# Layer 0's memory projection in plain fp32 in a two-layer streaming encoder step, with its loads reordered

## The chip, the cores and the metric

The kernel runs on one core of a Trainium2 chip. The time is the device time of one execution in microseconds (us), with all inputs and outputs in HBM. Three executions of the kernel before took 2020.75, 2020.86 and 2020.9 us.

## What is computed

```python
for l in range(2):                                  # two layers
    z = x @ W_in[l]                                 # 512 prompt tokens + 32 sample tokens, width 2048
    mk, mv = split(mem @ W_mem_kv[l])               # 256 memory tokens, 4 key heads and 4 value heads of 128
    outs = fox(z), band(z), swa(z), cross(mq, mk, mv)   # four groups of four heads
    x = layer_norm(ALPHA * x + (concat(outs) * silu(gate)) @ W_out[l])
# x is layer-normed once before the first layer; mk and mv are outputs too
```

Everything is fp32 at the interface. The change touches `mem @ W_mem_kv[0]` and what runs beside it: the loads and the first layer norm of x.

## The kernel before, in words

All weights are stored as tiles of 128 output columns: `wt[n]` is 128 partitions x 16 contraction chunks x 128 columns, 1 MB, and goes into one of two slots of `WR`. A layer begins with eight such tiles for the memory (`MEM_TILES`), then come the heads' tiles.

A matrix product of fp32 precision is made of three products in fp32r, a reduced format that TensorE takes in one step. ScalarE casts a weight tile to its high part `WH` (`w_hi`, L730), VectorE subtracts it to get the low part `WL` (`w_lo`, L1046), and the memory is split in the same way into `MTH` (`mem_hi`, L859) and `MTL` (`mem_lo`, L1248). `mem_tile` (L672) then issues 48 matmuls of 128x128 weights against 256 columns: high x high, low x high, high x low, 16 chunks each, into one bank of `GB`. ScalarE copies the bank to `MT` (`mem_done`, L907) and issues the store of a key head. Value heads are transposed by `turn_mem` (L638).

Each engine runs an order written out by hand: `PE_PLAN`, `ACT_PLAN` and `DVE_PLAN`. Beside the eight memory tiles, layer 0 does the first layer norm with tokens as rows: five row blocks `XT` (the last, 32 rows, is `XTS`) are loaded (L374), summed (`first_sum`, L916 on ScalarE, L1311 on VectorE), squared (`first_square`, L923), turned to 1/deviation (`first_seed` L929/L931, `first_rstd` L1324 to L1328) and normalised (`first_norm`, L1333). Then TensorE transposes them chunk by chunk inside memory tiles 5, 6 and 7 (`turn_x`, L648 and L654, at the places that `TURNED` names), VectorE scales them (`first_affine`, L1351), and ScalarE casts them and stores them (`first_hi`, L942 and L944), two chunks for each `("x", g)` of the plan. After tile 7, `forget` (L619, L626) computes the forget gates from all 16 casted chunks; it waits for `xh` to count 16.

In `mem_done(0, j)` ScalarE waits for the end of tile j, casts the weights of tile j + 2 (which waits for their load), and only then copies tile j's bank:

```python
act.wait_ge(zd, n + 2)
if j < MEM_TILES - 1:
    w_hi(n + 2, s, l * (LT // 2) + j // 2 + 2)
...
act.copy(MT[:, s, :], GB[:, 2 * s, 0:NMEM]).then_inc(zf[s], 1)
```

All loads here are issued by SyncE, in order; a wait holds up everything behind it. A slot of `WR` may be loaded again when `w_lo` of the tile in it is done (`lo`). POOL issues the stores of the value heads. Tile n begins when its bank of two is free (`zf`), so ScalarE may be one tile behind. The order of loads is: tile 0's weights, the memory in quarters, row block 0, tile 1, row block 1, tile 2 (after tile 0 is split), row blocks 2, 3 and 4, the identity and norm vectors, tile 3, the other constants, and the later tiles in a loop.

Layer 1 does its memory tiles in the same way, beside another norm; the change leaves them alone but for their counts.

Of the kernel before, what the change touches and what calls it, by code (L numbers as in the profile page):

```python
# [14 lines left out]
KC = DM // P  # L15
# [4 lines left out]
NMEM = 256  # L20
# [20 lines left out]
WT = O0 + KC  # L41
# [9 lines left out]
class Group:  # L51
    def __init__(self, blocks, cached, own, place, sink=False):
# [23 lines left out]
    [("w1", 0), ("sum", 0), ("square", 0), ("mem", 0), ("square", 1), ("square", 2), ("mem", 1), ("square", 3),  # L76
     ("square", 4), ("seed", 0), ("mem", 2), ("mem", 3), ("mem", 4), ("sample", 0), ("x", 0), ("x", 1), ("x", 2),
     ("mem", 5), ("x", 3), ("x", 4), ("x", 5), ("mem", 6), ("x", 6), ("x", 7), ("mem", 7)],
# [3 lines left out]
    [("w1", 0), ("sum", 1), ("sum", 2), ("w", 0), ("sum", 3), ("sum", 4), ("w", 1), ("rstd", 0), ("norm", 0),  # L82
     ("w", 2), ("norm", 1), ("norm", 2), ("norm", 3), ("norm", 4), ("w", 3), ("sample", 0), ("x", 0), ("x", 1),
     ("w", 4), ("x", 2), ("mv", 4), ("x", 3), ("w", 5), ("x", 4), ("x", 5), ("mv", 5), ("x", 6), ("x", 7), ("w", 6),
     ("low", 0), ("low", 1), ("low", 2), ("low", 3), ("low", 4), ("mv", 6), ("low", 5), ("low", 6), ("low", 7),
     ("mv", 7)],
# [55 lines left out]
def encoder_step(nc, wt, wff, bff, x_t, mem_t, fox_k, fox_v, fox_logf, band_k, band_v, swa_k, swa_v, mem_k, mem_v,  # L142
                 rel_pad, sinks, ln_gt, ln_bt, ident_d, causal_d, swa_mask_d, cos_d, sin_d,
                 y_o, fk_o, fv_o, fl_o, bk_o, bv_o, sk_o, sv_o, mk_o, mv_o):
    with ExitStack() as ctx:
# [14 lines left out]
        def sem(name):  # L160
            return ctx.enter_context(nc.semaphore(name))
# [96 lines left out]

        hi = sem("hi")
# [93 lines left out]

        def pt_col(j):
            return PT[:, P * j:P * (j + 1)]
# [10 lines left out]
        def _(sp):  # L366

            sp.dma_start(WR[:, 0, :, :], wt[0]).then_inc(raw[0], 16)
            for p in range(NQ):
                cs = slice(p * KC // NQ, (p + 1) * KC // NQ)  # L370
                sp.dma_start(MTR[:, cs, :], mem_t[:, cs, :]).then_inc(ld_mem[p], 16)
# [31 lines left out]

            for l in range(DEPTH):
                load_weights(2 if l == 0 else 0, O0 // 2, l * LT, l * WT)
                for h in range(2):
                    load_weights(0, KC // 2, l * LT + O0 + h * KC, l * WT + O0)
# [8 lines left out]
        def _(pe):  # L416
# [240 lines left out]
            def mem_tile(l, j, turned, middle=None):  # L657
                s, n = j % 2, l * LT + j
                pe.wait_ge(hi, n + 1)
                pe.wait_ge(zf[s], l * (LT // 2) + j // 2 + 1)  # L660
                for i, (w, x) in enumerate(((WH, MTH), (WL, MTH), (WH, MTL))):
                    if i == 1:
                        pe.wait_ge(lo, n + 1)
                    for k in range(KC):
                        at = i * KC + k
                        if j == 0 and k % (KC // NQ) == 0 and i != 1:
                            pe.wait_ge(m_lo if i else m_hi, NQ * l + k // (KC // NQ) + 1)
                        if at % 3 == 0 and at // 3 in turned:
                            turn_x(turned[at // 3])
                        if at == 3 * KC // 2 and middle is not None:  # L670
                            middle()
                        mm = pe.matmul(GB[:, 2 * s, 0:NMEM], w[:, s, k, :], x[:, k, :],  # L672
                                       start=(at == 0), stop=(at == 3 * KC - 1))
                mm.then_inc(zd, 1)

            pe.wait_ge(s_one, 1)
            for l in range(DEPTH):
# [7 lines left out]
                for kind, i in PE_PLAN[l]:  # L685
                    if kind == "mem":
                        mem_tile(l, i, TURNED.get(i, {}) if l == 0 else {}, last_sums if l and i == 0 else None)
# [36 lines left out]
        def _(act):  # L724
# [221 lines left out]
            w_hi(0, 0, 1)  # L946
            mem_hi(0)
            act.wait_ge(s_one, 1)
            act.preload_act_table_set("natural_log_exp_and_others")
            for l in range(DEPTH):  # L950
                for kind, i in ACT_PLAN[l]:
                    if kind == "w1":
                        w_hi(1, 1, 1)
                    elif kind == "sum":
# [86 lines left out]
        def _(dve):  # L1041
# [202 lines left out]
            def mem_lo(r):  # L1244
                for p in range(NQ):
                    cs = slice(p * KC // NQ, (p + 1) * KC // NQ)
                    dve.wait_ge(m_hi, NQ * r + p + 1)
# [115 lines left out]
            for released, count in ((zd, 1), (zf[0], 1), (zf[1], 1), (tf, 1), (gd, 1), (oe, 2), (pv, 2), (sm1, 1),  # L1363
                                    (sm2, 2)):
                dve.sem_inc(released, count)
# [3 lines left out]
            w_lo(0, 0)  # L1369
            mem_lo(0)  # L1370
            chains = {"first": Chain(dve, c_dx), "ln": Chain(dve, c_dl), "ff": Chain(dve, c_df), "pair": Chain(dve, c_dc)}
            heads_chain = chain
            for l in range(DEPTH):
                chain = chains["ln" if l else "first"]
                for kind, i in DVE_PLAN[l]:
                    if kind == "w1":
                        w_lo(1, 1)
                        first_mean(0)
# [316 lines left out]
```

## Time and profile before

| | us |
|---|---|
| three executions, median | 2020.86 |
| the profiled execution | 2021.17 |
| its span in the profile | 2019.4 |
| TensorE busy (98% of the span) | 1981.5 |
| VectorE busy | 1049.7 |
| ScalarE busy | 705.0 |

The span is what the hardware profiler records of one execution; about 1.8 us of the time lies around it. Positions below are us from the start of the span. Of a matmul, the duration includes its way through the array, so consecutive ones overlap: the distance from one to the next is what a stream costs, and the chain of waits shows that. The granted clock is 1.00 where TensorE runs at 2.4 GHz and 0.50 where it runs at 1.2 GHz.

### The profile page before, as it was taken

Reading aid. Unit: us, or ns where it says so; the run is one execution under the profiler, and the core shown is the slowest. Engines: PE = TensorE matmul, PEld = TensorE weight load, DVE = VectorE, ACT = ScalarE, POOL = GpSimd, SP = SyncE. Lnnn points to the kernel's source line nnn. Section 1 sums busy time; section 2 is a strip of 40 time slices with the busy share of each in tenths; the row PEclk is TensorE's granted clock in tenths of the full one; section 3 lists DMA queues with packets and bytes.
Section 4 is the critical chain, followed back from the end, with each engine's and each line's share of the span. In section 5 each row is a group of like instructions: output and inputs, shape, how many; then the busy total and the mean of one; then the engine's idle time right before and its main releaser. Section 6 shows DMA issues by size and latency. Waiting matters only on the chain.

```text
span 2019.4 us, 38302 instructions
## 1 busy us (share of the span) xinstructions
PE 1981.5 (98%) x15868; PEld 1956.7 (97%) x15868; DVE 1049.7 (52%) x1649; ACT 705.0 (35%) x1053; POOL 133.4 (7%) x238
## 2 busy tenths in 40 slices
PE   7999999999999999999999999999999999999995
PEld 6999999999999999999999999999999999999995
DVE  6743333333465445677884333434335545557776
ACT  6423232222233233544573222222222322344444
POOL 0110000000000000000001101000000000000000
PEclk9999999999999999999999999999999999999998
DMA  8632232222222222555664323222222222225563
GB/s 305 241 131 93 98 107 85 99 99 90 94 71 99 69 90 82 201 201 194 220 216 142 107 88 107 84 100 86 91 105 90 79 72 87 100 72 211 182 225 133
DMA packets 55050, 254.75 MB, mean 126 GB/s; under 512 B 9468, under 2 KB 19324, under 8 KB 30864
## 3 DMA queue, kind: packets, MB, share of 16 engines
q1 hardware_dynamic: 31184, 202.68, 28.0%
q0 software_dynamic: 13344, 36.51, 5.3%
q10 hardware_dynamic: 10432, 14.29, 1.9%
q8 instruction: 65, 1.06, 0.2%
q14 instruction: 25, 0.20, 0.0%
HBM read 228.36 MB, written 27.70 MB: 127 GB/s over the span
## 4 chain that ended last, share of the span: by engine, by line
PE 96%; DVE 2%; DMA 1%; ACT 1%; issue 0%; SPq 0%; ACTq 0%; DVEq 0%
PE GB L426 62%; PE GB L450 19%; PE AB L479 3%; PE AB L522 3%; PE GB L672 3%; PE AB L490 2%; DMA WR<-in_wt 1%; PE AB L619 1%; DVE WL L1046 1%; PE AB L527 0%; PE AB L507 0%; PE AB L530 0%; PE AB L626 0%; PE AB L654 0%; PE AB L494 0%; DVE OY L1287 0%
## 5 line engine op out<-in xcount | busy, mean ns | idle before, releaser
L730 ACT CAST WH<-WR 128x2048 fp32r<-128x2048 f32 x184 | 351.2, 1908 | 725.7 <-PE GB L426 531.3
L1046 DVE TENSOR_TENSOR WL<-WR,WH 128x2048 fp32r<-128x2048 f32 x184 | 421.4, 2290 | 344.3 <-ACT WH L730 344.0
L426 PE MATMUL GB<-XH,WH 128*128 128x272 f32 x3328 | 458.1, 290 | 0.0
L426 PE MATMUL GB<-XL,WH 128*128 128x272 f32 x3328 | 451.3, 287 | 0.0
L426 PE MATMUL GB<-XH,WL 128*128 128x272 f32 x3328 | 451.2, 287 | 0.0
L426 PEld LDWEIGHTS GB<-XL,WH 128*128 128x128 f32 x3328 | 431.2, 189 | 0.0
L426 PEld LDWEIGHTS GB<-XH,WL 128*128 128x128 f32 x3328 | 431.2, 189 | 0.0
L426 PEld LDWEIGHTS GB<-XH,WH 128*128 128x128 f32 x3328 | 429.5, 188 | 1.5
L450 PE MATMUL GB<-XH,WL 128*128 128x272 f32 x1024 | 149.7, 288 | 3.3 <-DVE WL L1046 3.3
L450 PE MATMUL GB<-XL,WH 128*128 128x272 f32 x1024 | 151.3, 288 | 0.0
L450 PE MATMUL GB<-XH,WH 128*128 128x272 f32 x1024 | 149.2, 287 | 0.0
L743 ACT ACTIVATE S<-S,nmx 128x256 f32<-128x256 f32 (+8 forms) x160 | 83.8, 524 | 174.4 <-DVE nmx L1088 172.7
L450 PEld LDWEIGHTS GB<-XH,WL 128*128 128x128 f32 x1024 | 136.4, 188 | 4.2 <-DVE WL L1046 4.2
L450 PEld LDWEIGHTS GB<-XL,WH 128*128 128x128 f32 x1024 | 137.1, 188 | 0.5
L450 PEld LDWEIGHTS GB<-XH,WH 128*128 128x128 f32 x1024 | 136.3, 188 | 0.0
L1153 DVE SCALAR_TENSOR_TENSOR SPL<-GB,SPL 128x544 fp32r<-128x544 f32 x24 | 17.3, 720 | 141.6 <-ACT SPL L789 141.6
L1119 DVE SCALAR_TENSOR_TENSOR GA<-ES,GB 128x544 f32<-128x544 f32 x30 | 21.6, 719 | 119.6 <-ACT ES L758 119.6
L1105 DVE COPY PT<-AB 128x512 f32<-128x512 f32 x64 | 40.2, 670 | 68.8 <-PE AB L490 68.8
L1088 DVE TENSOR_REDUCE nmx<-S 128x1 f32<-128x256 f32 (+8 forms) x160 | 69.8, 436 | 5.5
L479 PE MATMUL AB<-SPL 128*128 128x256 f32 (+6 forms) x552 | 70.3, 279 | 0.0
L479 PEld LDWEIGHTS AB<-SPL 128*128 128x128 f32 (+1 forms) x552 | 64.7, 164 | 4.1
L522 PE MATMUL AB<-PT,V 128*128 128x128 f32 x560 | 67.6, 275 | 0.0
(178 smaller groups left out, 1496.3 us busy)
## 6 DMA issues: line engine op xcount, KB each, us to landing
WR<-in_wt SPq DMA_DIRECT2D x184, 1024.0 KB, 4.8
XR<-out POOLq DMA_DIRECT2D x64, 136.0 KB, 2.9
out<-OY ACTq DMA_DIRECT2D x24, 272.0 KB, 2.2
out<-OY ACTq DMA_DIRECT2D x8, 544.0 KB, 5.4
out<-KT POOLq DMA_DIRECT2D x16, 272.0 KB, 2.5
out<-VT POOLq DMA_DIRECT2D x16, 272.0 KB, 2.3
XT<-in_x_t SPq DMA_DIRECT2D x4, 1024.0 KB, 13.5
BI<-nc_rows POOLq DMA_DIRECT2D x8, 400.0 KB, 4.2
```

What stands on the lines that cost most here:

```text
L426: mm = pe.matmul(GB[:, 2 * s + hf, 0:HALF], w[:, s, k, :], x[:, k, hf * HALF:(hf + 1) * HALF], start=(k == 0 and i == 0), stop=(k == KC - ...
L450: mm = pe.matmul(GB[:, 2 * s + hf, 0:HALF], w[:, s, k, :], x[:, k, half(hf)], start=(at == 0), stop=(at == 3 * KC - 1))
L479: mm = pe.matmul(AB[0:r, b, at:at + w], q[:, t0:t0 + r], k, start=(p == 0), stop=(p == 2))
L490: mm = pe.transpose(AB[:, j // 4, P * (j % 4):P * (j % 4 + 1)], S[:, at:at + P], ident[:, :])
L522: mm = pe.matmul(AB[:, 3, P * i:P * (i + 1)], V[:, kb, :], pt_col(j), start=(b == 0), stop=(b == len(g.blocks[i]) - 1))
L672: mm = pe.matmul(GB[:, 2 * s, 0:NMEM], w[:, s, k, :], x[:, k, :], start=(at == 0), stop=(at == 3 * KC - 1))
L730: act.copy(WH[:, s, :, :], WR[:, s, :, :]).then_inc(hi, 1)
L743: act.activation(s, s, ACT.Exp, bias=nmx[0:r, i:i + 1], accum_out=esum[0:r, i:i + 1]).then_inc(ex, 1)
L1046: dve.tensor_tensor(WL[:, s, :, :], WR[:, s, :, :], WH[:, s, :, :].bitcast(F32), ALU.subtract).then_inc(lo, 1)
L1088: dve.tensor_reduce(nmx[0:r, i:i + 1], S[0:r, at:at + w + g.sink], AX_X, ALU.max, negate=True).then_inc(mk, 1)
L1105: dve.tensor_copy(PT[:, 512 * b:512 * b + w], AB[:, b, 0:w]).then_inc(pte, 1)
L1119: dve.scalar_tensor_tensor(split2(GA[:, :]), split2(ES[:, :]), 1.0, z2(s), ALU.add, ALU.mult) \
```

## The change

Layer 0's memory tiles are no longer split. A new `first_mem_tile` multiplies the loaded weights `WR` with the loaded memory `MTR`, 16 matmuls per tile, both operands plain fp32. ScalarE's `w_hi` and `mem_hi` and VectorE's `w_lo` and `mem_lo` of these tiles are gone; `hi` and `lo` are set to 8 at the start instead. The splits of tiles 8 and 9, the first of the heads, stay where they were (in `mem_done(0, 6)`, and in the first head).

A slot of `WR` is now free when its tile's matmuls are done: the loads of tiles 2 to 9 wait for `zd`. The first load becomes four quarters, each followed by a quarter of the memory; tile 1 goes ahead of row block 0; tile 3 goes ahead of the identity and norm vectors. `turn_x` keeps its positions in `TURNED`, which now count the 16 matmuls of a tile (before: every third of 48).

```diff
@@ ACT_PLAN and DVE_PLAN, layer 0
-    [("w1", 0), ("sum", 0), ("square", 0), ("mem", 0), ("square", 1), ("square", 2), ("mem", 1), ("square", 3),
...
+    [("sum", 0), ("square", 0), ("mem", 0), ("square", 1), ("square", 2), ("mem", 1), ("square", 3), ("square", 4),
...
-    [("w1", 0), ("sum", 1), ("sum", 2), ("w", 0), ("sum", 3), ("sum", 4), ("w", 1), ("rstd", 0), ("norm", 0),
-     ("w", 2), ("norm", 1), ("norm", 2), ("norm", 3), ("norm", 4), ("w", 3), ("sample", 0), ("x", 0), ("x", 1),
-     ("w", 4), ("x", 2), ("mv", 4), ("x", 3), ("w", 5), ("x", 4), ("x", 5), ("mv", 5), ("x", 6), ("x", 7), ("w", 6),
...
+    [("mean", 0), ("sum", 1), ("sum", 2), ("sum", 3), ("sum", 4), ("rstd", 0), ("norm", 0), ("norm", 1), ("norm", 2),
+     ("norm", 3), ("norm", 4), ("sample", 0), ("x", 0), ("x", 1), ("x", 2), ("mv", 4), ("x", 3), ("x", 4), ("x", 5),
+     ("mv", 5), ("x", 6), ("x", 7), ("w", 6), ("low", 0), ("low", 1), ("low", 2), ("low", 3), ("low", 4), ("mv", 6),
...
@@ sync
-            sp.dma_start(WR[:, 0, :, :], wt[0]).then_inc(raw[0], 16)
             for p in range(NQ):
-                sp.dma_start(MTR[:, cs, :], mem_t[:, cs, :]).then_inc(ld_mem[p], 16)
+                done = ld_first[p] if p < NQ - 1 else raw[0]
+                sp.dma_start(WR[:, 0, quarter(p), :], wt[0][:, quarter(p), :]).then_inc(done, 16)
+                sp.dma_start(MTR[:, quarter(p), :], mem_t[:, quarter(p), :]).then_inc(ld_mem[p], 16)
             def load_first(n):
-                sp.wait_ge(lo, n - 1)
+                sp.wait_ge(zd, n)
                 sp.dma_start(WR[:, n % 2, :, :], wt[n]).then_inc(raw[n % 2], 16)
+            sp.dma_start(WR[:, 1, :, :], wt[1]).then_inc(raw[1], 16)
             load_rows(0)
-            sp.dma_start(WR[:, 1, :, :], wt[1]).then_inc(raw[1], 16)
             load_rows(1)
             load_first(2)
             load_rows(2)
             load_rows(3)
             load_rows(4)
+            load_first(3)
             for dst, src in ((ident, ident_d), (gT, ln_gt), (bT, ln_bt)):
                 sp.dma_start(dst[:, :], src).then_inc(s_turn, 16)
-            load_first(3)
...
+            for n in range(4, MEM_TILES + 2):
+                load_first(n)
@@ tensor
+            def first_mem_tile(j, turned):
+                s = j % 2
+                if j:
+                    pe.wait_ge(raw[s], 16 * (j // 2 + 1))
+                pe.wait_ge(zf[s], j // 2 + 1)
+                for k in range(KC):
+                    if j == 0 and k % (KC // NQ) == 0:
+                        p = k // (KC // NQ)
+                        if p < NQ - 1:
+                            pe.wait_ge(ld_first[p], 16)
+                        else:
+                            pe.wait_ge(raw[0], 16)
+                        pe.wait_ge(ld_mem[p], 16)
+                    if k in turned:
+                        turn_x(turned[k])
+                    mm = pe.matmul(GB[:, 2 * s, 0:NMEM], WR[:, s, k, :], MTR[:, k, :], start=(k == 0),
+                                   stop=(k == KC - 1))
+                mm.then_inc(zd, 1)
@@ scalar, mem_done
-                if j < MEM_TILES - 1:
+                if MEM_TILES - 2 - l * MEM_TILES <= j < MEM_TILES - 1:
                     w_hi(n + 2, s, l * (LT // 2) + j // 2 + 2)
@@ scalar and vector, before the plans
-            w_hi(0, 0, 1)
-            mem_hi(0)
...
-            w_lo(0, 0)
-            mem_lo(0)
```

## Rows read from the trace of the kernel before

**Rows 1.** The page: the chain that ended last, its shares by engine.
```profile
PE 96%; DVE 2%; DMA 1%; ACT 1%; issue 0%; SPq 0%; ACTq 0%; DVEq 0%
```

**Rows 2.** The chain of waits, first 140 us: start, us, what.
```profile
4.24 11.97 DMA WR<-in_wt
...
20.50 11.69 DMA WR<-in_wt
...
48.98 1.15 PE AB L648 x16
...
70.43 0.43 PE AB L654 x4
70.86 3.20 PE GB L672 x27
74.06 0.22 PE GB L638 x2
74.28 7.94 PE AB L619 x64
```

**Rows 3.** The chain at a plain fp32 product of 128 columns; the timeline at one of 272.
```profile
139.09 2.23 PE AB L522 x20
...
918.17 1.08 PE L605 MATMUL AB<-LNB,ones 128*128 128x272 f32 x4
```

**Rows 4.** Stretches: length, busy us of PE, PEld, DVE, ACT, POOL, PEclk, DMA share, GB/s.
```profile
26.00:27.00 1.00, 1.00 (x9) 0.79 (x7) 0.97 (x2) 1.00 (x1) 0.00 (x0) 1.00 1.15 211
...
36.00:37.00 1.00, 1.00 (x6) 1.00 (x6) 0.49 (x1) 1.00 (x3) 0.00 (x0) 0.50 0.04 16
```

**Rows 5.** Timeline, 8 to 20 us: start, duration, engine, line, what [idle before].
```profile
8.90 4.74 PE L672 MATMUL GB<-MTH,WH 128*128 128x256 f32 x16 [8.90 <-ACT MTH L859]
10.08 1.05 ACT L859 CAST MTH<-MTR 128x1024 fp32r<-128x1024 f32 x1 [0.20 <-DMA MTR<-in_mem_t]
...
11.32 1.04 ACT L859 CAST MTH<-MTR 128x1024 fp32r<-128x1024 f32 x1 [0.19 <-DMA MTR<-in_mem_t]
...
13.44 2.30 PE L672 MATMUL GB<-MTH,WL 128*128 128x256 f32 x16
```

**Rows 6.** The same view, 20 to 50 us.
```profile
23.71 2.29 DVE L1311 TENSOR_REDUCE XST<-XT 128x1 f32<-128x2048 f32 x1 [0.80 <-DMA XT<-in_x_t]
...
28.44 2.15 PE L672 MATMUL GB<-MTH,WL 128*128 128x256 f32 x16 [1.44 <-DVE WL L1046]
...
34.58 3.60 PE L672 MATMUL GB<-MTH,WH 128*128 128x256 f32 x16 [2.09 <-ACT MT L907]
...
43.73 3.85 DVE L1333 TENSOR_SCALAR XT<-XT,XST 128x2048 f32<-128x2048 f32 x3
```

**Rows 7.** The same view, ScalarE, 65 to 75 us.
```profile
67.23 1.90 ACT L730 CAST WH<-WR 128x2048 fp32r<-128x2048 f32 x1
69.04 0.36 ACT L907 COPY MT<-GB 128x256 f32<-128x256 f32 x1
...
71.75 0.63 ACT L942 CAST XH<-OY 128x512 fp32r<-128x512 f32 x1 [0.54 <-DVE OY L1351]
```

**Rows 8.** The loads of one line: tile 4's, 8's and 9's, issue and landing.
```profile
L402 SPq DMA_DIRECT2D WR<-in_wt x1: 348/348/348, 28.6 to 28.6; - x1
DMA to landing us min/median/max: 8.2/8.2/8.2
...
L402 SPq DMA_DIRECT2D WR<-in_wt x1: 333/333/333, 57.8 to 57.8; - x1
DMA to landing us min/median/max: 5.8/5.8/5.8
...
L402 SPq DMA_DIRECT2D WR<-in_wt x1: 333/333/333, 64.0 to 64.0; - x1
DMA to landing us min/median/max: 6.6/6.6/6.6
```

**Rows 9.** The same view, tile 2's load, issued at 10.24.
```profile
DMA to landing us min/median/max: 11.0/11.0/11.0
```

More of the change, by code:

```diff
@@ L75 @@
 ACT_PLAN = [
-    [("w1", 0), ("sum", 0), ("square", 0), ("mem", 0), ("square", 1), ("square", 2), ("mem", 1), ("square", 3),
-     ("square", 4), ("seed", 0), ("mem", 2), ("mem", 3), ("mem", 4), ("sample", 0), ("x", 0), ("x", 1), ("x", 2),
-     ("mem", 5), ("x", 3), ("x", 4), ("x", 5), ("mem", 6), ("x", 6), ("x", 7), ("mem", 7)],
+    [("sum", 0), ("square", 0), ("mem", 0), ("square", 1), ("square", 2), ("mem", 1), ("square", 3), ("square", 4),
+     ("seed", 0), ("mem", 2), ("mem", 3), ("mem", 4), ("sample", 0), ("x", 0), ("x", 1), ("x", 2), ("mem", 5), ("x", 3),
+     ("x", 4), ("x", 5), ("mem", 6), ("x", 6), ("x", 7), ("mem", 7)],
     [("seed", 0), ("mem", 0), ("late", 0), ("mem", 1), ("x", 0), ("mem", 2), ("x", 1), ("x", 2), ("x", 3), ("mem", 3),
@@ L257, in encoder_step @@
         o_y = sem("o_y")
+        ld_first = [sem(f"ld_first{p}") for p in range(NQ - 1)]
         hi = sem("hi")
@@ L352, in token_rows, with quarter @@
             return XT[0:r, i, :] if i < NT - 1 else XTS[0:r, :]
+        def quarter(p):
+            return slice(p * KC // NQ, (p + 1) * KC // NQ)
         def pt_col(j):
@@ L655, in turn_x, with mem_tile @@
                 mm.then_inc(x_turn, 1)
-            def mem_tile(l, j, turned, middle=None):
+            def first_mem_tile(j, turned):
[16 more added lines that the diff above has]
+                mm.then_inc(zd, 1)
+            def mem_tile(l, j, middle=None):
                 s, n = j % 2, l * LT + j
@@ L666, in mem_tile @@
                         if j == 0 and k % (KC // NQ) == 0 and i != 1:
-                            pe.wait_ge(m_lo if i else m_hi, NQ * l + k // (KC // NQ) + 1)
-                        if at % 3 == 0 and at // 3 in turned:
-                            turn_x(turned[at // 3])
+                            pe.wait_ge(m_lo if i else m_hi, NQ * (l - 1) + k // (KC // NQ) + 1)
                         if at == 3 * KC // 2 and middle is not None:
@@ L685, in _ @@
                 for kind, i in PE_PLAN[l]:
-                    if kind == "mem":
-                        mem_tile(l, i, TURNED.get(i, {}) if l == 0 else {}, last_sums if l and i == 0 else None)
+                    if kind == "mem" and l == 0:
+                        first_mem_tile(i, TURNED.get(i, {}))
+                    elif kind == "mem":
+                        mem_tile(l, i, None if i else last_sums)
                     elif kind == "forget":
@@ L951, in _ @@
                 for kind, i in ACT_PLAN[l]:
-                    if kind == "w1":
-                        w_hi(1, 1, 1)
-                    elif kind == "sum":
+                    if kind == "sum":
                         first_sum(i)
@@ L1360, in _ @@
             dve.memset(esum[:, :], 1.0)
-            for released, count in ((zd, 1), (zf[0], 1), (zf[1], 1), (tf, 1), (gd, 1), (oe, 2), (pv, 2), (sm1, 1),
+            for released, count in ((hi, MEM_TILES), (lo, MEM_TILES), (zd, 1), (zf[0], 1), (zf[1], 1), (tf, 1), (gd, 1), (oe, 2), (pv, 2), (sm1, 1),
                                     (sm2, 2)):
@@ L1375, in _ @@
                 for kind, i in DVE_PLAN[l]:
-                    if kind == "w1":
-                        w_lo(1, 1)
-                        first_mean(0)
+                    if kind == "mean":
+                        first_mean(i)
                     elif kind == "sum":
```

8 lines of the change are left out of this document (3 added, 5 removed).

## The prediction, made before the changed kernel was run

> **What bounds the kernel now.** I read the chain of waits first. By the page TensorE holds 96% of it [rows 1], so all that counts is when TensorE can go on. The change acts on the first 75 us, so I took the chain of that part [rows 2]. Up to 32.2 us it runs through loads of weight tiles: tile 1's, landed at 16.21, and tile 3's, issued at 20.50 and landed at 32.19. From 48.98, when the last row block is normalised, it is all TensorE: the transposes and memory tiles 5 to 7, then `forget` at 74.28. From there on the changed kernel has the same instructions in the same order. So the result is the start of `forget` in the changed kernel against 74.28, and the profiled execution moves by that. That one took 2021.17 us, 0.3 above the median of 2020.86; I add the difference to the median.
>
> The stretches say what bounds each part: through the first 33 us the DMA engines are full: 512 KB take 1.24 us where the rows are long [rows 5], 423 GB/s, and the worst microsecond moves half of that, still at a full share [rows 4]. After 49 TensorE is full.
>
> **The prices.**
> - An fp32r matmul of 256 columns: 27 in 3.20 us, 118.5 ns [rows 2]. A tile of 48 takes 5.7 us.
> - A plain fp32 matmul of 256 columns: no row has it, but rows lie on both sides [rows 3]. At 128 columns (L522, 10 matmuls in a head of four causal blocks) the chain shows 20 instructions in 2.23 us: each matmul is executed as two, 111.5 ns each, of which 106.7 is two cycles a column at 2.4 GHz. At 272 columns (L605, two matmuls) there are four instructions in 1.08 us; less the 0.39 that one takes through the array, three distances are 0.69, 230 ns each, of which 227 is two cycles a column. At 256 that gives 213 + 3 to 5, twice: 435 ns. The upper end is 474, two halves that each cost two fp32r matmuls of 118.5. I take 437: 7.0 us a tile, 1.3 more than now; the upper end is 7.6. At 1.2 GHz a matmul takes 1024 cycles, 853 ns.
> - The transposes: four for a chunk take 0.44, the sample's 1.15, a value head's two 0.22 [rows 2]. They are unchanged.
> - ScalarE: weight cast 1.90, bank copy 0.36, chunk cast 0.63 [rows 7].
>
> **Part by part, to the end of tile 4.** The quarters: the casts of the memory quarters wait for their loads and begin 1.24 us apart (10.08, 11.32), for 512 KB [rows 5], so 768 KB (a weight and a memory quarter) land every 1.86. The last memory quarter still lands at 11.3, as the bytes before it are the same; so the first pair lands at 5.7. TensorE starts there instead of at 8.90 [rows 5].
>
> The Trainium skill, "DMA: Bandwidth & Descriptors", section "Bandwidth", speaks against quarters: it wants DMAs of 1 MB or more. By its fit of about 2 us fixed cost per DMA an estimate would put tile 0 some 6 us later for three extra DMAs, if the costs added up; the 1.24 us between quarters of 512 KB is shorter than one such cost, so the trace disagrees with adding them up.
>
> Tile 0 begins at the low clock: in the present kernel matmuls from 8.90 on run slow until about 13.4, 4.6 us [rows 5]. From 5.7 to 10.3 at 853 ns that makes 5.4 matmuls, the other 10.6 at 437 take 4.6: end 14.9. The quarters come faster than they are used. Tile 1's weights land 1 MB earlier than now, 16.2 - 2.4 = 13.8, so tile 1 runs 14.9 to 21.9. Tile 2's load is issued at 15.0 instead of 10.24, but its place in the queue is the same and it is not idle by then: it lands at 10.24 + 11.0 = 21.2 as now [rows 9]. Tile 2: 21.9 to 28.9.
>
> Tile 3's load is issued at 22 (now 20.50), which still finds row blocks 3 and 4 queued. It now stands ahead of the three small-row loads, whose neighbourhood is that slow microsecond [rows 4]. It lands between 29.4 (32.2 less 1.1 MB of full rate and the loss) and 32.2 (nothing gained); I take 30.5. So TensorE idles 1.6 us, and tile 3 runs 30.5 to 37.5. Tile 4's load is issued when tile 2 ends, 28.9, now at 28.57, with the same bytes ahead of it; it landed at 36.8 [rows 8] and will again. Tile 4: 37.5 to 44.5, and tile 5 starts at 44.5. Now tile 4 ends at 47.7.
>
> SyncE is not the hold-up: behind its wait for tile 1's end (21.9) stand ten small issues, over by 27, before its wait for tile 2's end at 28.9. Behind its wait for tile 0 (15.0) stand row blocks 2 to 4, whose turn in the full queue comes after 21.
>
> Does the norm keep up? Row block 2 lands at 23.7 as now [rows 6]; blocks 3 and 4 are not later. VectorE, with no splits, sums blocks 2, 3 and 4 back to back, 2.3 each, to 30.7; ScalarE squares at 2.2 each to about 33.5; root and the five norms (1.28 each [rows 6]) end at 41.5. That is 7 us earlier than now and 3 before tile 5 needs them. The bank copies of tiles 1 and 2, behind squares in ScalarE's order, come at 28.7 and 34.6, both before tiles 3 and 4 need the banks.
>
> **Tiles 5 to 7.** TensorE work from the start of tile 5: 3 tiles 21.0, sixteen chunks 7.0, the sample 1.15, two value heads 0.44: 29.6, so tile 7 ends at 74.1, the next value head at 74.3. By TensorE alone the two kernels tie: what the loads and the norm give (3.2) goes into 1.3 more per tile.
>
> But a wait moves. In `mem_done(0, 6)` ScalarE casts tile 8's weights ahead of the copy of tile 6's bank and of the last four chunk casts, all of which `forget` needs. Tile 8's load now waits for the split of tile 6, issued at 57.8, landed 63.6, before tile 6's end; the cast starts at 67.23 [rows 7, 8]. In the changed kernel the load waits for tile 6's matmuls: tile 5 takes 7.0 + 1.15 + 6 x 0.44 = 10.8, a value head 0.2, tile 6 9.6, so it is issued at 44.5 + 20.6 = 65.1. Loads among the stores of the normed x took 5.8 and 6.6 [rows 8]; 6.2 gives 71.3. Then cast 1.9, copy 0.4, four casts 2.6, handovers 0.1: 76.3. `forget` starts at 76.3 instead of 74.28: +2.0. What is behind it on ScalarE, tile 7's copy, is needed only in the middle of `forget`. VectorE's split of tile 8 (2.3 from 73.2) and its low parts keep ahead of L626. Tile 9's load, from 74.1, is needed after 90.
>
> The removed work on ScalarE (8 weight casts and 4 memory casts) and on VectorE gives nothing beyond the earlier norm: neither is on the chain elsewhere.
>
> Sum for the likeliest case: 2020.9 + 2.0 = 2022.9, own range 2021.2 to 2024.
>
> **The rivals.**
> 1. *The wait at `forget` is not the last* (an engine bound in its place). Tile 3's load lands at 29.4, tile 5 starts at 43.8, tile 8's load takes 5.0: ScalarE ends at 43.8 + 20.6 + 5.0 + 5.0 = 74.4, TensorE 73.6. Result 2020.1 to 2021.0. For it: tile 3's place is better. Against: the stores of x are in flight just then, so 5.0 is under both rows.
> 2. *The clock drops in the gap before tile 3.* An idle of 1.44 us before 28.44 was followed by 16 fp32r matmuls in 2.15; one of 2.09 before 34.58 by 16 in 3.60 and a granted clock of 0.50 [rows 4, 6]. My gap of 1.6 lies between. A drop costs tile 3 about 1.6: 2024.5.
> 3. *Slower beyond doubt: tile 3's load is as late as now.* Its issue after TensorE's tile 1, behind the full queue, gains nothing and it lands at 32.2. The gap of 3.3 us is then past the one that dropped the clock: tile 3 ends at 32.2 + 8.6 = 40.8, tile 5 starts at 47.8, 3.3 later than in the sum: 2026.2. It decides once the landing is past about 31.
> 4. *The plain product is dearer*, 474 ns: tile 0 ends at about 15.3, then 7.6 each with no gap before tile 3, so tile 5 starts at 45.7 and the end of tile 6 moves by 1.2 more: +2.4 on the sum, 2025.3. Against it: both rows of plain products have 3 to 5 ns over their cycles.
> 5. *The change does not do what it says*, as fp32 operands might still be taken in one step: tiles of 16 x 118.5 = 1.9 us, loads would bound, and tile 5 would start at the norm's end, 41.5. Then 14.3 of work, `forget` near 62, if ScalarE's end did not hold it at tile 8's load: 2010 or so. The doubled instructions of rows 3 speak against it clearly.
> 6. *The quarters cost what a lone load does.* Tile 8's load took 5.8 for 1 MB [rows 8], 3.3 over its 2.5 of transfer at 423 GB/s; three more of them in a row put tile 0 and all behind it up to 9.9 later: 2032. Against it: the 1.24 us [rows 5]. By the page named above this rival would come to 6 later, as an estimate.
>
> **Chances.** Likeliest case 0.42; rival 1 0.16; rival 2 0.20; rival 3 0.13; rival 4 0.05; rival 5 0.03; rival 6 0.01. A measurement here tells 0.2%, 4.0 us, from no change: faster is below 2016.8, slower above 2024.9. The likeliest case, rival 1 and most of rival 2 are within. Slower takes rivals 3, 4 and 6 and a little of rival 2: 0.20; faster rival 5: 0.03; same 0.77. The range goes from 2019.9 (rival 1 with half a us to spare) to 2025.8, which takes in the dearer product and leaves rival 6 and most of rival 3 outside.
>
> **What would show it.** L672's successor with 32 instructions a tile, 218 ns apart; TensorE's first matmul near 5.7; tile 3 waiting for its load until 30.5 after 1.6 idle, granted clock 1.00 behind it; tile 5 starting at 44.5 with no wait for XTS; then ScalarE's cast of tile 8 waiting for its load until about 71, and TensorE idle for some 2 us before L619's successor, released by the last chunk cast. Wrong would be a `forget` that starts right behind the value head's transposes, tiles of another length than 7.0 at the full clock, or any difference that arises after `forget`.

## The result, and the profile after

The changed kernel takes 2027.69 us, the median of eight executions (2024.34 to 2030.36); the kernel before takes 2020.82 beside them (2020.1 to 2021.9). The ratio is 1.0033, 95% interval 1.0024 to 1.0043: slower by 6.9 us (0.3%) where 2.0 was predicted, and above the range. The profiled execution took 2030.16 with a span of 2028.4, so it is one of the long ones, 9.0 over the profiled execution of before.

The chain of waits of the changed kernel, first 100 us (start, us, what), answers to [rows 2]:

```profile
5.21 11.09 DMA WR<-in_wt
...
16.34 7.19 PE GB L678 x32
...
23.55 11.41 DMA WR<-in_wt
...
35.00 17.57 PE GB L678 x68
...
72.31 6.32 DMA WR<-in_wt
...
78.70 1.91 ACT WH L755
...
82.84 0.23 DVE WFF L1319
...
83.11 8.10 PE AB L625 x64
```

`forget` (L625) starts at 83.11 where it started at 74.28: 8.8 of the 9.0 us are there. The span less that start is 1945.3 now and 1945.1 before, so nothing differs behind it. Ahead of it stand three loads: tile 1's, tile 3's (issued at 23.55, landed at 34.96) and tile 8's.

The timeline of the changed kernel on TensorE and the two ends of its wait at `forget` (start, duration, engine, line, what, idle before):

```profile
6.85 9.10 PE L678 MATMUL GB<-MTR,WR 128*128 128x256 f32 x32 [6.85 <-DMA MTR<-in_mem_t]
...
16.34 7.17 PE L678 MATMUL GB<-MTR,WR 128*128 128x256 f32 x32 [0.39 <-DMA WR<-in_wt]
...
23.80 7.17 PE L678 MATMUL GB<-MTR,WR 128*128 128x256 f32 x32 [0.28 <-DMA WR<-in_wt]
...
35.00 17.57 PE L678 MATMUL GB<-MTR,WR 128*128 128x256 f32 x68 [4.03 <-DMA WR<-in_wt]
...
43.90 1.33 DVE L1354 TENSOR_SCALAR XTS<-XTS,XST 32x2048 f32<-32x2048 f32 x1
...
78.70 1.90 ACT L755 CAST WH<-WR 128x2048 fp32r<-128x2048 f32 x1 [5.79 <-DMA WR<-in_wt]
...
80.63 2.29 DVE L1067 TENSOR_TENSOR WL<-WR,WH 128x2048 fp32r<-128x2048 f32 x1 [2.51 <-ACT WH L755]
...
83.11 8.10 PE L625 MATMUL AB<-XH,WFF 128*4 128x272 f32 x64 [1.69 <-DVE WFF L1319]
```

A tile is 32 instructions and takes 7.0 us, as predicted. The norm (XTS, done at 45.2) is ready long before it is needed. TensorE idles 4.03 us before tile 3, and behind that the first 68 instructions take 17.57 instead of the 14.9 that they take at full clock in the runs below. The stretches (length, busy of PE, PEld, DVE, ACT, POOL, granted clock, DMA share, GB/s) show the two things at work: a DMA queue that is full and moves half, and then the clock at half:

```profile
26.00:27.00 1.00, 1.00 (x7) 0.87 (x6) 0.74 (x1) 0.06 (x1) 0.00 (x0) 1.00 1.25 279
31.00:32.00 1.00, 0.00 (x0) 0.00 (x0) 1.00 (x1) 0.12 (x1) 0.00 (x0) 1.00 1.01 229
36.00:37.00 1.00, 1.00 (x4) 0.79 (x3) 0.00 (x0) 1.00 (x1) 0.00 (x0) 0.50 1.12 447
```

Issue and time to landing of row blocks 3 and 4 together, and of tile 3 (16.83 + 13.7 = 30.5; 17.30 + 15.2 = 32.5; 23.55 + 11.4 = 35.0):

```profile
L378 SPq DMA_DIRECT2D XT<-in_x_t x1: 432/432/432, 16.8 to 16.8; - x1
L378 SPq DMA_DIRECT2D XTS<-in_x_t x1: 429/429/429, 17.3 to 17.3; - x1
DMA to landing us min/median/max: 13.7/14.5/15.2
...
L382 SPq DMA_DIRECT2D WR<-in_wt x1: 340/340/340, 23.5 to 23.5; - x1
DMA to landing us min/median/max: 11.4/11.4/11.4
```

From row block 2 (landed at 26.2) on, the 2.36 MB of row blocks 3 and 4 and of tile 3 took 8.7 us, where 5.6 would do at 423 GB/s. Row block 3 came 4.3 behind row block 2, row block 4 2.0 behind that, tile 3's weights another 2.4. At full rate it is 2.5, 0.6 and 2.5: all of the loss lies at the two row blocks.

### The profile page after: what moved, and what is told of

It reads as the page before. It is cut to its first block, busy times and chain, and to the rows that moved or that the text cites. A ratio compares the mean times of both kernels' runs of the same rounds, so it can differ in the third digit from the quotient of the medians.

```text
span 2028.4 us, 38003 instructions
## 1 busy us (share of the span) xinstructions
PE 1991.0 (98%) x15740; PEld 1957.3 (96%) x15740; DVE 1029.0 (51%) x1637; ACT 685.3 (34%) x1040; POOL 134.9 (7%) x238
## 4 chain that ended last, share of the span: by engine, by line
PE 96%; DMA 1%; DVE 1%; issue 0%; ACT 0%; SPq 0%; ACTq 0%; DVEq 0%
PE GB L432 62%; PE GB L456 18%; PE AB L485 3%; PE AB L528 3%; PE GB L695 2%; PE GB L678 2%; PE AB L496 2%; DMA WR<-in_wt 1%; PE AB L625 1%; PE AB L533 0%; DVE WL L1067 0%; PE AB L513 0%; PE AB L536 0%; PE AB L632 0%; PE AB L500 0%; DVE OY L1308 0%
## 5 line engine op out<-in xcount | busy, mean ns | idle before, releaser
L755 ACT CAST WH<-WR 128x2048 fp32r<-128x2048 f32 x176 | 336.0, 1909 | 713.8 <-PE GB L432 529.1
L1067 DVE TENSOR_TENSOR WL<-WR,WH 128x2048 fp32r<-128x2048 f32 x176 | 403.5, 2293 | 336.4 <-ACT WH L755 335.9
L1174 DVE SCALAR_TENSOR_TENSOR SPL<-GB,SPL 128x544 fp32r<-128x544 f32 x24 | 17.3, 720 | 141.0 <-ACT SPL L814 141.0
L678 PE MATMUL GB<-MTR,WR 128*128 128x256 f32 x256 | 63.7, 400 | 11.7 <-DMA MTR<-in_mem_t 6.8
L1126 DVE COPY PT<-AB 128x512 f32<-128x512 f32 x64 | 40.2, 670 | 67.4 <-PE AB L496 67.4
L678 PEld LDWEIGHTS GB<-MTR,WR 128*128 128x128 f32 x256 | 49.5, 201 | 20.1 <-issue 7.7
```

Of the source, the lines that this page charges most:

```text
L678: mm = pe.matmul(GB[:, 2 * s, 0:NMEM], WR[:, s, k, :], MTR[:, k, :], start=(k == 0), stop=(k == KC - 1))
L755: act.copy(WH[:, s, :, :], WR[:, s, :, :]).then_inc(hi, 1)
L1067: dve.tensor_tensor(WL[:, s, :, :], WR[:, s, :, :], WH[:, s, :, :].bitcast(F32), ALU.subtract).then_inc(lo, 1)
L1126: dve.tensor_copy(PT[:, 512 * b:512 * b + w], AB[:, b, 0:w]).then_inc(pte, 1)
```

## The experiments

The theory after the result had three parts: (1) the loads around row blocks 3 and 4 clog the queue, so tile 3's load is late; (2) the idle that follows also costs half the clock; (3) tile 8's load, cast and split are the last link at `forget`. The kernel before gave 2021.4, 2021.6, 2021.1 and 2021.3 beside the four groups of runs (e1 to e4, e5 to e8, e9 to e12, the last three). Where a trace is quoted, it is one execution.

**The changed kernel again.**

> The changed kernel again, for a second trace. The eight times of it run from 2024.3 to 2030.4, those of the kernel before from 2020.1 to 2021.9, and the one trace (2030.2) has 4.0 us of idle before tile 3 and 6 us at half clock behind it. Theory A (the landing of tile 3's load and the half clock that follows vary from run to run): the trace of a faster run shows a shorter stretch at half clock or a shorter idle before tile 3, and forget starts later than 74.3 by as much as the time is over 2021. Rival B (the spread is somewhere behind forget): the start of forget is again near 83.1 whatever the time.

Median 2028.16 (2026.1 to 2029.9, six executions). The trace (2028.28) has tile 3's load at 34.0, 3.41 us of idle, the first 68 instructions in 16.63 and `forget` at 81.26; the span less that is 1945.2 again. So between two executions 1.85 us of `forget` are 0.9 of load and 0.9 of clock. Theory A holds.

**Keeping TensorE busy through the idle.**

```diff
+                if j == 3:
+                    for k in range(8):
+                        pe.matmul(AB[:, 3, 0:NMEM], MTR[:, k, 0:P], MTR[:, k, :], start=True, stop=True)
```

> Eight plain fp32 matmuls of the memory with itself, into a bank that nobody reads, stand before tile 3's wait (3.5 us of work in the 4.0 us of idle); the rest is the changed kernel. Theory A (the idle costs twice: 4 us itself and about 2.8 by the half clock behind it): tile 3 takes 7.0 instead of 9.8 us, forget starts 2.8 earlier, about 80.3, and the time is 2 to 3 lower and less spread. Rival B (what held the clock down is the kind of work or the start of the run, not the idle): tile 3 takes 9 to 10 us again and nothing moves.

2026.21 (2025.5 to 2029.7). Its timeline:

```profile
29.75 3.62 PE L667 MATMUL AB<-MTR 128*128 128x256 f32 x16
33.20 14.93 PE L681 MATMUL GB<-MTR,WR 128*128 128x256 f32 x68
```

The 68 instructions come in 14.93 with no stretch at half clock: the clock cost 1.7 to 2.6 us in the two traces above, and the time falls by 2.0. (Tile 3 begins when the extra matmuls end, 0.2 behind its load.) The fall against the first eight executions is 1.5. Theory A, with the size of the drop at the lower end.

**The small loads behind tile 4's load.**

```diff
             load_first(3)
+            load_first(4)
             for dst, src in ((ident, ident_d), (gT, ln_gt), (bT, ln_bt)):
...
-            for n in range(4, MEM_TILES + 2):
+            for n in range(5, MEM_TILES + 2):
```

> The eleven small loads (identity, norm vectors, masks, cos, sin, gate weights, cached gates) are issued behind tile 4's load instead of in front of its wait, so that none is issued before tile 2 is done. Theory A (the small loads, many short rows, issued right behind tile 3's load, hold up row block 3, row block 4 and tile 3's load though these stand ahead of them; 26 to 32 us moved 197 to 295 GB/s): that stretch moves 400 or more, tile 3's load lands near 32 instead of 35, the idle before tile 3 is 1 us instead of 4, the clock is not lost, forget starts 5 us earlier (78), time 2024 to 2025. Rival B (row block 4, 32 rows in 32 partitions, or the store of the first key head is what slows the queue): row block 3 still lands over 4 us after row block 2, tile 3's load near 35, the time as in the changed kernel.

The trace has row block 3 at 28.0, 3.1 behind row block 2 (24.9), row block 4 1.6 behind that, and tile 3's load lands at 32.2:

```profile
6.65 22.97 PE L679 MATMUL GB<-MTR,WR 128*128 128x256 f32 x96 [6.65 <-DMA MTR<-in_mem_t]
32.23 14.94 PE L679 MATMUL GB<-MTR,WR 128*128 128x256 f32 x68 [2.61 <-DMA WR<-in_wt]
```

From row block 2 on it is 7.3 us. With the small loads in their place it was 8.7, 8.1, 8.0 and 8.4 in the traces of the changed kernel, the changed kernel again, the busy idle and the late cast (below), so the small loads cost 0.7 to 1.4 there, by one trace without them. `forget` is at 77.75, 5.4 earlier than in the first trace; but this execution (2025.09) had no half clock after 2.61 idle, and others did worse: median 2026.97, from 2024.95 to 2030.43. Half right: the queue is relieved by 0.7 to 1.4, not 3. Of the rest of that trace's gain, 1.3 is an earlier row block 2 (24.9 instead of 26.2), with the same bytes ahead of it, and 2.6 the clock's luck.

**Tile 8's cast and split last.**

```diff
-     ("x", 4), ("x", 5), ("mem", 6), ("x", 6), ("x", 7), ("mem", 7)],
+     ("x", 4), ("x", 5), ("mem", 6), ("x", 6), ("x", 7), ("w8", 0), ("mem", 7)],
...
-     ("mv", 5), ("x", 6), ("x", 7), ("w", 6), ("low", 0), ("low", 1), ("low", 2), ("low", 3), ("low", 4), ("mv", 6),
+     ("mv", 5), ("x", 6), ("x", 7), ("low", 0), ("low", 1), ("low", 2), ("low", 3), ("low", 4), ("mv", 6),
+     ("w", 6), ("low", 5), ("low", 6), ("low", 7), ("mv", 7)],
...
```

(`mem_done(0, 6)` no longer casts tile 8's weights; `("w8", 0)` does.)

> ScalarE casts tile 8's weights behind the last chunk casts instead of ahead of tile 6's bank copy, and VectorE splits them behind the low parts of the gate weights and of the first chunks. Theory A (tile 8's load, landed at 78.6, is the last link: cast, split, low gate weights, then forget at 83.1, 2 us after TensorE is free): forget starts right behind the value head's transposes, 1.9 us earlier, and the time is 1.9 lower. Rival B (the split of tile 8, now later, makes the first head wait, or the wait at forget has another releaser): the time stays, with an idle of TensorE at forget or before the first head's low products.

2025.18 (2022.85 to 2027.78). Tile 3's idle (3.68) and the half clock (16.63) are as in the second trace of the changed kernel, and tile 5 starts 0.34 earlier than there; `forget` follows on TensorE's own work at 79.16 instead of 81.26. The rest, 1.8 us, is what the tail cost. Theory A. (The median fell by 3.0; the trace shows 2.1 of it.)

**Tile 0's weights whole; and all loads in the old order.**

```diff
-            for p in range(NQ):
-                done = ld_first[p] if p < NQ - 1 else raw[0]
-                sp.dma_start(WR[:, 0, quarter(p), :], wt[0][:, quarter(p), :]).then_inc(done, 16)
+            sp.dma_start(WR[:, 0, :, :], wt[0]).then_inc(raw[0], 16)
+            for p in range(NQ):
...
```

> The changed kernel with tile 0's weights loaded whole, as before; the memory's quarters and all else as changed. Theory A (the weight quarters, 2 KB a partition, cost queue time: all loads behind them land about 2.5 us later than their bytes did before): row block 2 lands near 23.8 instead of 26.3 and tile 3's load 2 us earlier, near 32.5; TensorE starts at 7.6 instead of 6.8 and reaches the end of tile 0 at 16 to 17; the idle before tile 3 shrinks from 4 to 2 us, forget starts 2 earlier, 80 to 81, time about 2026. Rival B (the first transfers start late for another reason, the quarters are free): row block 2 lands at 26 again and forget starts 1 us later than in the changed kernel.

> The changed kernel with the loads exactly in the order and size of the kernel before; the plain fp32 tiles and the earlier release of the weight slots stay. Theory A (new order and quarters cost more than they give): tile 1's load lands near 16.2, tile 0 ends at 16 to 17, tile 3's load lands at about 32.5 to 33.5, forget starts at 80 to 81, the time is 1 to 2 under the changed kernel and 5 to 6 over the kernel before. Rival B (the new order pays): forget starts later than 83, time above 2028.

2026.23 (ten executions) and 2028.65 (five). The traces are alike:

```profile
7.62 23.50 PE L675 MATMUL GB<-MTR,WR 128*128 128x256 f32 x96 [7.62 <-DMA MTR<-in_mem_t]
33.08 16.63 PE L675 MATMUL GB<-MTR,WR 128*128 128x256 f32 x68 [1.96 <-DMA WR<-in_wt]
```

```profile
7.53 23.59 PE L675 MATMUL GB<-MTR,WR 128*128 128x256 f32 x96 [7.53 <-DMA MTR<-in_mem_t]
33.13 16.63 PE L675 MATMUL GB<-MTR,WR 128*128 128x256 f32 x68 [2.01 <-DMA WR<-in_wt]
```

Without the quarters TensorE starts 0.8 later, but tile 1's load lands at 13.7 in e5, where the quarters have it at 16.3 (first trace) or 15.0 (e3). Row block 1, with the same bytes ahead of it, lands at 18.7, as in the kernel before, and at 21.3 or 19.9 with quarters. Little of that is kept: tile 0 ends at 17.3 and only then is tile 2's load issued, with nothing but row block 1 left in the queue; it lands at 22.4 and 22.2 (23.8 and 22.4 with quarters), and tile 3's at 33.0 and 33.1. `forget` starts at 80.4 and 80.1. So the quarters start TensorE earlier and delay the loads behind them, and are no gain. In the traces, putting tiles 1 and 3 ahead moves nothing either: from row block 2 to tile 3's load it is 8.2 us with the three small loads behind tile 3 (e5) and 8.2 with them ahead (e6). That e6's five executions were longer than e5's ten with the same trace stays open; both traces have the half clock, and more of e5's executions may have gone without it.

**Row block 4 behind tile 3.**

```diff
-            load_rows(4)
             load_first(3)
+            load_rows(4)
+            load_first(4)
```

> The changed kernel with row block 4 (32 rows, in 32 partitions) loaded behind tile 3, and the small loads behind tile 4. With the small loads late alone, 27 to 29 us still moved 240 to 250 GB/s, tile 3's load landed at 32.2 and TensorE idled 2.6. Theory A (what is left of the slow stretch is row block 4): tile 3's load lands near 30.5, the idle is 1 us, the clock stays, forget starts near 76, time 2023 to 2024. Rival B (it is the store of the first key head, or nothing to do with one load): row block 3 still takes over 3 us behind row block 2, tile 3's load lands at 31.5 or later, no gain over the small loads alone.

2024.71, and nine of ten executions between 2024.3 and 2026.0, `forget` at 78.00. But the mechanism is neither's in full. Its timeline and stretches:

```profile
32.16 14.94 PE L679 MATMUL GB<-MTR,WR 128*128 128x256 f32 x68 [2.10 <-DMA WR<-in_wt]
```

```profile
28.00:29.00 1.00, 1.00 (x6) 0.90 (x5) 0.98 (x1) 1.00 (x1) 0.00 (x0) 1.00 1.00 401
30.00:31.00 1.00, 0.06 (x1) 0.00 (x0) 0.46 (x2) 0.57 (x2) 0.00 (x0) 1.00 0.38 107
```

Row block 3 lands 2.7 behind row block 2, nearly at full rate; now tile 3's load, which stands *ahead* of row block 4, lands 4.1 behind row block 3, at 32.1, and row block 4 at 33.0. The slow stretch follows row block 4 in the queue and takes what is beside it along. It isn't the store of the first key head either, the other cause that Rival B names: that store is issued at 22.6 and landed at 30.0, and 26 to 29 us moved 401 to 420 GB/s.

**A place for every tile.** The space of `WH` and `WL` is free during layer 0's memory tiles, so tiles 2 to 5 can be loaded without waiting for a slot; 6 and 7 wait for the ends of tiles 2 and 3, and 8 and 9 for those of tiles 0 and 1.

```diff
+        def place(n):
+            return {0: WR, 1: WHF, 2: WLF, 3: WHF, 4: WR}[n // 2][:, n % 2, :, :]
...
+                if n in (6, 7):
+                    sp.wait_ge(zd, n - 2)
+                if n in (8, 9):
+                    sp.wait_ge(zd, n - 6)
+                sp.dma_start(place(n), wt[n]).then_inc(raw[n % 2] if n > 7 else ld_w[n], 16)
```

> Plain fp32 tiles that never wait for a slot: tiles 2 to 5 go into the space of the high and low parts, which layer 0's memory tiles no longer use, 6 and 7 follow there, and tiles 8 and 9 are loaded as soon as tiles 0 and 1 are done. Loads: quarters, tile 1, row blocks 0 and 1, tile 2, row block 2, tile 3, row blocks 3 and 4, tiles 4 and 5, the small ones, and the rest. Theory A (the loss is made of the idle before tile 3, the half clock behind it and the late load of tile 8, and by TensorE's work alone the change ties): no idle over 1 us after tile 0, tile 5 starts at 44 to 45, forget at 74 to 75, time within 1 us of the kernel before and as little spread as it. Rival B (plain fp32 work itself is what costs): forget still starts after 77, with TensorE full all the way.

2026.03: the expectation failed. Tile 3's load was in time, but row block 3, between it and row block 4, landed at 32.4, 5 us behind tile 3's load. TensorE stopped before tile 4 for a bank: tile 2's copy stands on ScalarE behind row block 4's square and the seed. It idled 3.2 us and the clock fell (0.50 from 40 to 46). Mended, with row block 4 and tile 3 ahead of row block 3, and the copies of tiles 1 and 2 ahead of the squares:

```diff
             load_rows(2)
-            load_first(3)
-            load_rows(3)
             load_rows(4)
+            load_first(3)
+            load_rows(3)
...
-    [("sum", 0), ("square", 0), ("mem", 0), ("square", 1), ("square", 2), ("mem", 1), ("square", 3), ("square", 4),
-     ("seed", 0), ("mem", 2), ("mem", 3), ...
+    [("sum", 0), ("square", 0), ("mem", 0), ("square", 1), ("mem", 1), ("square", 2), ("square", 4), ("mem", 2),
+     ("square", 3), ("seed", 0), ("mem", 3), ...
```

> The kernel with a place for each tile, once more, with what stood in its way mended: there TensorE idled 3.2 us before tile 4, because row block 3 landed at 32.4, and tile 2's bank copy stood behind its square and the seed on ScalarE; the clock fell to half behind that. Now row block 4 and tile 3 are loaded ahead of row block 3, and the copies of tiles 1 and 2 stand ahead of the squares that wait. Theory A (the loss against the kernel before is made of idle, half clock and the late tile 8, and TensorE's work alone ties): no idle over 1 us after tile 1, tile 5 starts at 43.5 to 45, forget at 73.5 to 75, time within 1 us of the kernel before. Rival B (plain fp32 tiles cost more than that): forget after 77 with TensorE full.

2023.52 (eleven executions from 2021.58 to 2027.90); `forget` at 76.79. In the stretches the slow one has moved to where row block 4 is now, and the later ones are full; the timeline still has one idle:

```profile
27.00:28.00 1.00, 1.00 (x7) 0.87 (x6) 0.00 (x0) 0.00 (x0) 0.00 (x0) 1.00 0.82 172
33.00:34.00 1.00, 1.00 (x6) 0.87 (x6) 0.00 (x0) 0.97 (x1) 0.00 (x0) 1.00 1.07 443
```

```profile
32.75 7.17 PE L689 MATMUL GB<-MTR,WHF 128*128 128x256 f32 x32 [2.05 <-DMA WHF<-in_wt]
```

The idle before tile 3 is still 2.05 us, so the tie isn't reached: the median is 2.5 over the kernel before. But 76.79 less that idle is 74.7, against 74.28. With that load in time the two kernels would start `forget` within half a us of each other, as worked out from this trace and not measured. (The kernel before has 3.5 us of idle of its own in it, 1.44 inside tile 2 and 2.09 ahead of tile 3 [rows 6].)

**Row block 4's bytes twice.** The base is e3's kernel; the added load reads the same rows into space nobody reads, as 32 x 8 KB (the first line added, e9) or as 128 x 2 KB (the other, e10).

```diff
             load_rows(4)
+            sp.dma_start(JUNK[0:DEC, :], x_t[SEQ:TOK, :]).then_inc(s_junk, 16)
...
+            sp.dma_start(JUNK[:, 0:DM // 4], x_t[SEQ:TOK, :].rearrange("t (q c) -> (t q) c", q=4)).then_inc(s_junk, 16)
```

> The kernel with the small loads late, and behind row block 4 the same 256 KB once more, again 32 rows into 32 partitions, in space that nobody reads. In it row block 4 landed 2.1 us behind row block 3, for bytes that take 0.6, and 27 to 29 us moved 240 to 250 GB/s. Theory A (a load of 32 rows of 8 KB into 32 partitions takes 2 us of the queue whatever stands beside it): tile 3's load lands 2 later, near 34.3, and the idle before tile 3 is 4.5 us. Rival B (the slow microseconds at 26 to 32 have another cause, such as the store of the first key head): it lands 0.6 later, the price of the bytes.

> As the one before, but the 256 KB go as 2 KB into each of 128 partitions. Theory A (it is the 32 partitions): tile 3's load lands only 0.6 to 1.0 later than without it, near 33. Rival B (any further load costs as much): 34.3 as with 32 partitions.

Tile 3's load in e3, e9 and e10, all issued within 0.6 us of each other (22.48, 23.08, 22.86):

```profile
DMA to landing us min/median/max: 9.7/9.7/9.7
```

```profile
DMA to landing us min/median/max: 13.3/13.3/13.3
```

```profile
DMA to landing us min/median/max: 11.3/11.3/11.3
```

From row block 2's landing (24.9, 25.8, 25.3) to tile 3's it is 7.3, 10.6 and 8.8 us. So 256 KB into 32 partitions cost 3.3, the same bytes into 128 cost 1.5, and by rate they would be 0.6. Both more than expected, in the order of Theory A; each is one trace, where traces of like kernels differ by up to 0.8. In e9 row block 3, which stands ahead of both, came 4.8 behind row block 2, 1.7 more than in e3: as in e7, the load ahead is delayed too. Rows of 8 KB by themselves aren't slow, as the weights and the other row blocks have them in 128 partitions at full rate. Why few partitions hold up the neighbours stays open. The medians are 2029.8 and 2028.7.

**A warm start**, on top of e11's kernel.

```diff
+            for k in range(11):
+                pe.matmul(AB[:, 3, 0:P], ones[:, :], ones[:, :], start=True, stop=True)
             for l in range(DEPTH):
```

> The kernel of the run before, with eleven plain fp32 matmuls of 128 columns on the constant ones from 2.4 us on, while TensorE has nothing to do. Theory A (tile 0 takes 9 us instead of 7 because the clock is still at half): the clock is full from 7 us, tile 0 is then bound by its quarters and ends near 14 instead of 16; tile 1's load, landed at 15 to 16, takes most of it back, so forget starts 0.5 to 1 earlier. Rival B (the quarters bound tile 0 and not the clock): nothing moves.

2023.74: nothing in the median, against 2023.52. Tile 0 is then at full clock, yet waits for its quarters and ends at 15.1 (15.7 in e11), and tile 1's load lands at 15.5 (16.0). `forget` starts at 75.97, 0.8 earlier than in e11's trace, as Theory A has it; but 0.6 of it is that load, which TensorE doesn't hold up, and which differs as much between executions of one kernel. Undecided, and under 1 us either way.

**The cures together** (the diffs of e4 and e7, and the small loads behind tile 4)**, and the kernel before with its loads moved.**

> The changed kernel with the small loads behind tile 4, row block 4 behind tile 3, and tile 8's cast and split behind the last chunk. Alone, the first two together gave forget at 78.0 and 2024.7, the last gave 2 us. Theory A (they add up): forget at 76, time 2022.5 to 2023, about 1.5 above the kernel before, and the rest is the idle of 2 us that is left before tile 3. Rival B (the tail is taken up by another wait once the rest is mended): forget at 77.5 or later.

2023.39; `forget` at 76.33, right behind TensorE's own work, with 2.40 idle before tile 3 left. They add up: 78.0 less the tail's 1.8.

```diff
@@ the kernel before
             load_rows(4)
+            load_first(3)
+            load_first(4)
             for dst, src in ((ident, ident_d), (gT, ln_gt), (bT, ln_bt)):
...
-            load_first(3)
...
+            load_first(5)
             for l in range(DEPTH):
-                load_weights(2 if l == 0 else 0, O0 // 2, l * LT, l * WT)
+                load_weights(3 if l == 0 else 0, O0 // 2, l * LT, l * WT)
```

> The kernel before, with its split fp32r tiles, and only the eleven small loads moved behind tile 4's load. In it tile 3's load landed at 32.2, with 211 GB/s at 26 to 27 us, and the cast, two squares, the norm and TensorE followed in a chain to forget at 74.3. Theory A (the small loads slow the queue there too): tile 3's load lands near 31, the last row block is normalised 1 to 1.5 earlier, the half clock after the idle may go as well, forget starts at 72.5 to 73.5 and the time is 1 to 1.5 lower, about 2019.8 where the kernel before takes 2021.1. Rival B (the pace is set by ScalarE's and VectorE's own work): nothing moves.

And row block 4 behind tile 3:

```diff
-            load_rows(4)
             load_first(3)
+            load_rows(4)
             load_first(4)
```

> As the one before, with row block 4 issued behind tile 3's load too. Theory A (32 rows into 32 partitions hold up what stands beside them): tile 3's load lands 1 to 2 earlier again, near 29.5, row block 4 itself near 31, in time for VectorE's sum at 30.7; forget at 71.5 to 73, time another 0.5 to 1 lower. Rival B (row block 4 is then what is late): its sum and square come later, the norm ends later, time as with the small loads alone or above.

2020.79 and 2020.11 against 2021.31 for the kernel before. The stretches show whose the slow microsecond of [rows 4] is. With the small loads moved, it is still there:

```profile
26.00:27.00 1.00, 0.90 (x8) 0.69 (x6) 1.00 (x2) 1.00 (x1) 0.00 (x0) 1.00 1.03 213
```

With row block 4 behind tile 3's load as well, it has moved with row block 4:

```profile
26.00:27.00 1.00, 1.00 (x10) 0.88 (x8) 0.96 (x3) 1.00 (x1) 0.00 (x0) 1.00 0.97 410
...
28.00:29.00 1.00, 0.49 (x4) 0.50 (x5) 1.00 (x2) 1.00 (x1) 0.00 (x0) 1.00 0.89 197
```

The chain of the second:

```profile
20.58 10.41 DMA WR<-in_wt
...
31.06 1.90 ACT WH L732
...
46.38 1.25 DVE XTS L1335
...
73.07 7.94 PE AB L621 x64
```

Tile 3's load lands at 31.5 and 31.0, where Theory A had 31 and 29.5; the last row block is done 0.7 and 1.2 earlier, `forget` starts at 73.59 and 73.07. The gains of 0.5 and 1.2 us are under what an interval here can tell (ratios 0.9998, 0.9989 to 1.0007, and 0.9994, 0.9985 to 1.0003), though each of the second's eleven executions is below the median of before. It has the lowest median of the case, and its memory tiles are all split as before, none in plain fp32.

## Why the prediction was wrong, point by point

- **The place and the stages.** Right. All of the difference is ahead of `forget`, and nothing in ScalarE's and VectorE's relief paid later.
- **The price of a plain matmul.** Right: 68 instructions in 14.94 is 218 to 220 ns each, two for a matmul, 7.0 us a tile.
- **"The first pair lands at 5.7", "the bytes before it are the same".** Wrong by 1.1 us at the start, and by 2.5 for tile 1's load (16.3 instead of 13.8). A weight and a memory quarter together took 2.4 us on average instead of 1.86. The quarters of 2 KB a partition take more of the queue than their bytes; I took the rate of the memory's quarters [rows 5] for the weights' as well. Row block 2 landed at 26.2 instead of "at 23.7 as now", and tile 2 ended at 31.0, not 28.9. The Trainium skill ("DMA: Bandwidth & Descriptors", section "Bandwidth") wants DMAs of 1 MB or more; the traces agree in direction, 1.2 to 2.6 us on tile 1's load for three extra DMAs. The estimate of 6 adds up the fixed cost per DMA that this page of the Trainium skill gives, from a fit to loads issued by GpSimd.
- **"It lands between 29.4 and 32.2; I take 30.5."** This is the step that failed. Tile 3's load landed at 35.0 and 34.0 in the two traces of the changed kernel. Of the 4.5 us in the first, 2.5 were there at row block 2, and before it at row block 1 (21.3, against 18.7 where tile 0's weights are whole): they are the quarters'. 2.0 arose behind row block 2: 8.7 us from row block 2 to tile 3's load, where 6.8 was predicted and the kernel before had 8.5. I put the slow microsecond [rows 4] down to the three small loads, so that standing ahead of them would help. e5 against e6 and the kernel before with its small loads moved show that it doesn't, and e7, e9, e11 and the last run that the stretch is row block 4's. The lower end, "32.2 less 1.1 MB of full rate", had no ground either: the three loads that the change puts behind tile 3's are 112 KB, 0.3 us at 423 GB/s, and the other small ones stand behind it in both kernels. In the first trace the small loads weren't even moving in the slow part. Of the packets in 26 to 31 us, those of 8 KB are the row blocks' and the weights', the 90 of the other queue are the store's, and only 27, of under 512 B, are left:

```profile
DMA packets 255, 1.23 MB, mean 246 GB/s; under 512 B 27, under 2 KB 117, under 8 KB 117
...
q10 hardware_dynamic: 90, 0.09, 9.6%
```

- **"SyncE is not the hold-up", "over by 27".** Wrong, without harm: the small loads' issues lasted to 32.1, one of them 2.7 us, so tile 4's load was issued 1.1 after tile 2's end. It landed at 40.2, before tile 4 began.
- **Rival 3** was this mechanism, at 0.13, with its upper end drawn at what the kernel before had, 32.2. A load with later loads ahead of it can't have its old landing as the upper end; that is where the range was too low.
- **Rival 2**, the half clock, came with it: 2.6 us in the first trace, 1.9 in e9 and 1.7 in five others (16.63 for the first 68 instructions from tile 3 on, where 14.94 is the full clock).
- **The tail.** Right in place and nearly in size: tile 8's load took 6.3 (6.2 predicted), `forget` came 31.4 us after tile 5's start (31.8 predicted). The last link was the low part of the gate weights behind VectorE's split, which I had left out of what `forget` waits for; ScalarE's last cast ended only 0.1 earlier, so this cost no more than that. The four casts took 2.2, not 2.6.
- **The sum.** Tile 3 started 4.5 late, the two tiles from it took 2.7 longer, the tail 0.4 less: 6.8, by which `forget` missed 76.3 in the first trace.

## What to carry to other kernels

A load's landing is set by what shares the queue, behind it as well as ahead: read the stretches at full DMA share and low GB/s, and find which load travels with them, before giving a reordered load its old or a better time. When a change frees a slot later (here at the end of a tile's matmuls, instead of at its split), look at every consumer of the next load in that slot, down to the last one before the stage ends. And doing away with casts and splits pays only where those engines are on the chain (here up to 48.98, and there the loads took their place); the quarter more TensorE work that replaced them (7.0 us a tile instead of 5.7) is paid in full wherever TensorE is.

## What the runs showed that was not expected

- 256 KB as 32 rows of 8 KB into 32 partitions took 3.3 us of the queue, as 2 KB into 128 partitions 1.5, where 1 MB in rows of 8 KB took 2.5.
- The clock after an idle: after 1.96, 2.01 (e5, e6) and 2.09 [rows 6] the granted clock fell to 0.50; after 1.82, 2.05, 2.10, 2.40 and 2.61 (e12, e11, e7, e15, e3) it did not; after 3.2 to 5.9 it always did. A fall cost 1.7 us in the usual case. Between 1.96 and 2.61 us the length of the idle did not decide it, and that is a part of the spread of these kernels, up to 6 us against 2 to 3 for the kernel before.
- With many loads outstanding, SyncE's issues take 2.1 us instead of 0.4. In e8 (timeline of its DMA issues) the eighteenth, with 12 before it not yet landed, took 1.9, and the next four 2.1 each:

```profile
9.26 2.33 SPq L391 DMA_DIRECT2D WLF<-in_wt  x2
11.64 2.12 SPq L404 DMA_DIRECT2D ident<-in_ident  x1
13.79 2.11 SPq L404 DMA_DIRECT2D gT<-in_ln_gt  x1
```
